# Gate/up and down of a SwiGLU in one block, with another order of products and v loads

## The reference, cut to what matters

```python
def _layer(h, norm1_g, w_in, conv_w, pool_w, pool_scale, mix_g, w_out, norm2_g, w_gate_up, w_down):
    ...
    h = h + mix.astype(h.dtype) @ w_out
    v = _rmsnorm(h, norm2_g)
    gu = v @ w_gate_up
    gate, up = gu[..., :D_FF], gu[..., D_FF:]
    return h + (jax.nn.silu(gate) * up) @ w_down
```

## Time and profile before

| | us |
|---|---|
| median of 3 runs | 2558.04 |
| lowest and highest run | 2555.99, 2562.67 |
| profiled execution, its own time | 2564.68 |
| profiled execution, span from first to last instruction | 2563.1 |
| TensorE busy in the span | 2409.1 (94%) |
| first and last matmul start of gate/up | 905.00, 1990.36 |
| mean granted TensorE clock, share of full speed | 0.966 |

### The profile page before, as it was taken

How to read it: one execution, slowest core, us unless ns; L and a number is a source line. 1 busy time by engine, 2 the same in 40 slices (tenths; PEclk the granted TensorE clock), 3 DMA queues, 4 the chain that set the end, 5 groups by cost and what they waited for, 6 DMA issues and landing times. The chain is left out here.

```text
span 2563.1 us, 32577 instructions
## 1 busy us (share of the span) xinstructions
PE 2409.1 (94%) x11786; PEld 2157.3 (84%) x11786; DVE 1546.1 (60%) x2312; ACT 893.8 (35%) x1486; POOL 358.3 (14%) x509
## 2 busy tenths in 40 slices
PE   6999999788999689999999999999999599999997
PEld 4887888687887589999999999999999488888886
DVE  4443545555777375566765555855555375686775
ACT  4121211242443243333433333433333233454543
POOL 0110110015444001111010111111111000010101
PEclk9999999887999899999999999999999799999999
DMA  5556871365665447888656555555553786687874
GB/s 187 207 135 160 228 194 46 99 213 184 228 221 200 170 152 238 274 251 247 172 178 208 161 162 159 159 160 162 163 160 117 257 267 196 201 310 224 259 245 140
DMA packets 216058, 492.95 MB, mean 192 GB/s; under 512 B 27552, under 2 KB 60866, under 8 KB 207469
## 3 DMA queue, kind: packets, MB, share of 16 engines
q1 hardware_dynamic: 188301, 358.99, 43.1%
q0 software_dynamic: 27616, 132.11, 17.2%
HBM read 395.90 MB, written 164.31 MB: 219 GB/s over the span
## 5 line engine op out<-in xcount | busy, mean ns | idle before, releaser
L81 PE MATMUL gu_bank<-v_form_hi_sb,gu_hi_sb 128*128 128x428 f32 (+1 forms) x1848 | 658.8, 356 | 37.3 <-DVE gu_lo_sb L1604 29.5
L82 PE MATMUL gu_bank<-v_form_lo_sb,gu_hi_sb 128*128 128x428 f32 (+1 forms) x1848 | 658.1, 356 | 0.0
L83 PE MATMUL gu_bank<-v_form_hi_sb,gu_lo_sb 128*128 128x428 f32 (+1 forms) x1848 | 658.1, 356 | 0.0
L1604 DVE TENSOR_TENSOR gu_lo_sb<-gu_raw_sb,gu_hi_sb 128x512 fp32r<-128x512 f32 x462 | 313.5, 686 | 209.8 <-ACT gu_hi_sb L1556 209.8
L81 PEld LDWEIGHTS gu_bank<-v_form_hi_sb,gu_hi_sb 128*128 128x128 f32 x1848 | 347.5, 188 | 51.2 <-DVE gu_lo_sb L1604 38.2
L1556 ACT ACTIVATE gu_hi_sb<-gu_raw_sb 128x512 fp32r<-128x512 f32 x462 | 280.8, 626 | 255.9 <-PE gu_bank L83 246.1
L82 PEld LDWEIGHTS gu_bank<-v_form_lo_sb,gu_hi_sb 128*128 128x128 f32 x1848 | 347.6, 188 | 11.2
L83 PEld LDWEIGHTS gu_bank<-v_form_hi_sb,gu_lo_sb 128*128 128x128 f32 x1848 | 347.6, 188 | 10.8
L81 PE MATMUL down_bank<-down_hi_sb,act_hi_sb 128*128 128x512 f32 x770 | 301.6, 392 | 29.3 <-DVE act_lo_sb L1943 29.3
L82 PE MATMUL down_bank<-down_lo_sb,act_hi_sb 128*128 128x512 f32 x770 | 301.0, 391 | 0.0
L83 PE MATMUL down_bank<-down_hi_sb,act_lo_sb 128*128 128x512 f32 x770 | 301.0, 391 | 0.0
(11 more groups left out here) (187 smaller groups left out, 3299.8 us busy)
## 6 DMA issues: line engine op xcount, KB each, us to landing
gu_raw_sb<-gu_sums SPq DMA_DIRECT2D x264, 256.0 KB, 4.0
gu_raw_sb<-w_gu_q SPq DMA_DIRECT2D x198, 256.0 KB, 2.7
gu_sums<-w_gu_q POOLq DMA_DIRECT2D x24, 1408.0 KB, 14.5
down_raw_sb<-down_sums SPq DMA_DIRECT2D x132, 256.0 KB, 3.6
act_raw_sb<-act_forms SPq DMA_DIRECT2D x154, 192.0 KB, 3.6
down_raw_sb<-w_down_q SPq DMA_DIRECT2D x99, 256.0 KB, 3.3
w_raw_sb<-w_panels SPq DMA_DIRECT2D x40, 512.0 KB, 3.9
act_raw_sb<-act_forms SPq DMA_DIRECT2D x77, 256.0 KB, 4.3
```

The lines of the kernel that those rows point to most:

```text
L81: pe.matmul(out, w[0], x[0], start=first, stop=False, skip_group_check=True)
L82: pe.matmul(out, w[0], x[1], start=False, stop=False, skip_group_check=True)
L83: return pe.matmul(out, w[1], x[0], start=False, stop=last, skip_group_check=True)
L1604: dve.tensor_tensor(w_lo[:, s, :], raw[:, s, :], w_hi[:, s, :].bitcast(F32), ALU.subtract)\
```

## The change

gateup and down become one function, swiglu, with one block; row_ranges is the same and moves up. There are four parts.

**One weight ring.** Down's weights go through gate/up's raw, w_hi and w_lo: the ring's slot is that of GU_UNITS + u, and the semaphores count on (slot, unit_landed, w_lo_by). The loops over gate/up's units on ScalarE and VectorE, which work six units ahead, run on into down's splits. Down's first two products use banks chosen by acc, and TensorE waits there for the last readers of gate/up's banks (sl_made, c12_made, c21_made).

**Buffers laid over each other.** a_raw and a_hi lie where v_raw was, the first h tiles, y_tiles and junk where v_form_hi was, a_lo where v_form_lo was. So SP waits for the last v_form_lo before down's first activation tile and for all gate/up units (used) before the final weights and the h tiles, which still stand behind the eighth unit.

**Order of products.** TURN puts product 4 in the second place: 0, 4, 1, 2, 3, 5, 6. It holds for every iteration, for the order of weight tiles, of the v forms and of the sums.

**First v loads.** Only A11 is loaded ahead of the weights; A12 comes after the second weight tile, A21 and A22 after the fourth. Each quarter has a semaphore of its own.

```diff
-def gateup(nc, c, gu, dn, w_landed):
+def swiglu(nc, c, gu, dn, half, eps):
...
+    TURN = (0, 4, 1, 2, 3, 5, 6)
...
+        a_raw, a_hi = sb("act_raw", [P, SLOTS, UNIT]), sb("act_hi", [P, SLOTS, UNIT], F32R)
+        sb("gap_after_v_raw", [P, V_RAW - 2 * RING_SIZE])
+        h_even = sb("h_even", [P, 2, PAIRS[0][1], D])
+        y_tile, junk = sb("y_tiles", [P, 2, D]), sb("y_junk", [P, D])
+        sb("gap_after_v_form_hi", [P, V_FORM - (2 * PAIRS[0][1] + 3) * D])
+        a_lo = sb("act_lo", [P, SLOTS, UNIT], F32R)
...
             i, r = divmod(u, 2 * FORMS)
-            return i, r // 2, r % 2
-
-        def weights(u):
+            return i, TURN[r // 2], r % 2
...
+        def slot(u):
+            return (GU_UNITS + u) % SLOTS
...
+        def acc(g, i):
+
+            return bank[:, ((6, 7, 0, 3), (2, 5, 1, 4))[g % 2][i], :]
...
-            v_load(0)
+            v_load(0, A11)
             gu.all_made(sp)
...
+                if u == 1:
+                    v_load(0, A12)
+                elif u == 3:
+                    v_load(0, A21)
+                    v_load(0, A22)
...
+                if u == 0:
+                    sp.wait_ge(v_lo_made, FORMS * len(HALVES))
...
+                if u == SLOTS - 1:
+                    sp.wait_ge(used, GU_UNITS)
+                    sp.dma_start(gf[:, :], c["final_rows"]).then_inc(gf_landed, 16)
+                    h_load(0)
...
             def w_split(u):
-                if u >= UNITS:
+                if u >= GU_UNITS:
+                    splits(u - GU_UNITS)
                     return
...
-            for f in range(FORMS):
+            for q, f in enumerate(TURN):
                 v_split(0, f)
-                if 2 * f < AHEAD:
-                    w_split(2 * f)
-                    w_split(2 * f + 1)
-            for u in range(UNITS):
+                if 2 * q < AHEAD:
+                    w_split(2 * q)
+                    w_split(2 * q + 1)
+            for u in range(GU_UNITS):
...
                 v_split(k, f)
-                if f == 0:
+                if f == 4:
                     v_sum(k, D_)
                     v_sum(k, N6)
+                elif f == 1:
                     v_sum(k, E_)
-                elif f == 1:
                     v_sum(k, S3)
...
+                if j == 0 and g == 0:
+                    pe.wait_ge(sl_made, 2 * ITER)
+                elif j == 0 and g == 1:
+                    pe.wait_ge(c12_made, 2 * ITER)
+                    pe.wait_ge(c21_made, 2 * ITER)
+                elif j == 0:
                     pe.wait_ge(acc_read, reads_before(g - 1))
```

## The result

The changed kernel takes **2569.66 us** (median of 7 runs, 2567.51 to 2570.68) against 2559.47 (7 runs, 2555.99 to 2562.67): ratio 1.0035, interval 1.0025 to 1.0044. It is slower by about 10 us where 9.6 us of gain were forecast, outside the range (2534 to 2556) and on the side to which 5% were given.

What follows compares the result with a forecast made beforehand. TensorE, busy 94% of the span, was taken to bound the kernel with its own work plus standstills. -24.7 + 1.5 + 13.6 = -9.6 us gave 2548.4 from the median 2558.04; own range 2537 to 2555, with rivals A and B 2534 to 2556.

Steps and rivals of the forecast that it cites:

- part 1: First gate/up iteration: TensorE starts at 892.5, then stops until 913.65 for ScalarE's copy of product 0; +1.5 us.
- part 2: Ends of first and second third: TensorE waits 6.7 us for VectorE's reads of product 3 at each; +13.6 us together.
- usually it is free: Ordinary gate/up iterations: product 3's reads end 0.9 us before product 5 needs them, so the new order costs nothing.
- part 3: Gate/up to down: no wait at down's first matmul, 6.5 us at its ninth unit (unit 8); -24.7 us.
- T0: End of all gate/up products, 1990.55 in the trace of before; the forecast counts down's unit times from it.
- the copies behind them: Ends of two thirds: after the wait on product 3's reads, TensorE waits near 1 us on a copy of product 0.
- the slack of 0.9 us: Gate/up: time between the end of product 3's two reads and the start of the unit of product 5 needing them.
- Rival D: All gate/up iterations: product 5 right behind 3 makes each of 66 halves pay, 20 us, time 2568; chance 0.05.
- the opening sentence: Whole kernel: the span is TensorE's own work plus its standstills, and the change removes, adds or swaps no product.

Runs made afterwards that it cites:

- wave_4_to_11: Changed kernel with GpSimd's eight copy waves for down's weight sums in iterations 4 to 11 instead of 1 to 8: 2559.96 us, ratio 1.0005.
- before_banks: Kernel before with only down's PSUM banks in the changed kernel's order: 2562.09 us, ratio 1.0005.
- order_in_before: Kernel before with only the new order of products, v loads, sums and first splits; gate/up and down stay apart: 2584.65 us, ratio 1.0094.

## Why the prediction was wrong, step by step

| term | predicted us | measured us |
|---|---|---|
| part 1, first iteration | +1.5 | +2.3 |
| part 2, ends of two thirds | +13.6 | +6.9 and +6.7 |
| part 2, "usually it is free" | 0 | +7.3 |
| part 3, to down's ninth unit | -24.7 | -26.3 |
| spacing of down's matmuls | not counted | +5.3 |
| drain at the very end | not counted | +4.5 |

The measured column adds to +6.7 against the +6.0 of the spans. (6.9 is the first third's 14.2 less the 7.3 of wave_4_to_11; 26.3 is T0 + 52.9 before less T0 + 26.7 after.)

- **Part 1** was right in mechanism and nearly in size: 892.49 for 892.5, 913.78 for 913.65.
- **Part 2's priced step** was right: 6.68 and 6.55 us for 6.7. That the two places together agree to a tenth has luck in it, since the copies behind them were waited for 0.33 and 0.36 us and not near 1.
- **Part 3** was right: no wait at down's first matmul, 4.53 us at the ninth unit for 6.5, since its data landed 1.6 us earlier (the split at 2037.07, T0 + 23.6 for T0 + 25.2). The 26.3 has the spread of single executions in it: down of before waited 4.82 us at its ninth unit, the same instructions 2.61 us in before_banks and 3.32 in order_in_before; from their starts of that unit, T0 + 50.3 and 53.4, it would be 23.6 and 26.7.
- **The step that failed first** is "usually it is free". It took the slack of 0.9 us from an undisturbed iteration and asked only whether VectorE is late by its own work. The trace of before had the place: ScalarE 9.67 and VectorE 11.36 us at a late weight in iteration 2, harmless only because the reads behind it were product 5's. The new order puts product 3's there. Rival D named the mechanism but spread it over 33 iterations; it holds in the one where transfers meet. That D's 2568 lies near the measured 2569.66 is chance.
- **The second** is what part 3 took to be the price of a block's end. All 24.5 us before down's first matmul were put down as gained, though 4.5 of them were a drain that the joined block still makes, at its end.
- **The third** is the opening sentence that TensorE's own work does not change because no product does: the same matmuls were 1% further apart.

With only what was priced the sum would have been some 10 us of gain. The three unseen terms come to 17.1 us and turn it.

## What to carry to other kernels

When an order of work is changed, look in the trace of before for stalls that something hides, such as a transfer that VectorE waits for without TensorE noticing, and ask which reads the new order puts behind them. When two blocks are merged, what ended the first is not gone; look for its drain at the end of the merged one, and try one by hand where something runs beside it. When buffers are laid anew, compare the start-to-start time of the same matmuls before and after at the same clock: a gap of 64 bytes gave 5 us back here.

## What the runs showed that was not expected

The spacing of down's fp32 matmuls of 128x512 depends on where the buffers lie: 0.2264 us with all four of them at one remainder of 256 bytes, 0.2287 with act_hi and act_lo 64 bytes off it, while gate/up's matmuls of 128x428 did not change with the same shift. GpSimd's drains add up here: 4.54 + 2.01 us in two blocks, 6.51 in one, and 4.55 + 2.01 again with one drain put between; with the same transfers issued later the one drain was 4.79 and 4.22 us.
